# A dense block's norm steps put beside every second RWKV projection, and eight dense pieces moved into a gated product

## The reference

```python
# first block
o = diff_attention(...); y = gelu(s5_ssm(...))
y = y * sigmoid(y @ w_glu + b_glu)              # the gated product
y = rms_norm(y, ssm_out_g)
h_res = h_res + rms_norm(concat(o, y) @ w_out, post_mix_g)
h = rms_norm(h_res, pre_ffn_g)                  # "mix norm": both lines
f = (silu(h @ w_gate) * (h @ w_up)) @ w_down
x = h_res + rms_norm(f, post_ffn_g)
# second block
proj = rms_norm_2(x, norm_mix_w) @ w_in         # 14 tiles of RWKV columns, then retention
y = concat(retention(...), rwkv7_mix(...))
x = x + y @ w_o
x = x + (silu(rms_norm_2(x, norm_ffn_w) @ w_gate) * ...) @ w_down
```

## Time and profile before

| | us |
| --- | --- |
| median of 3 runs | 3587.25 (3585.57 to 3601.52) |
| the profiled execution | 3581.31 |
| its span, first to last instruction | 3579.3 |

### The profile page before, as it was taken

The page is one execution under the profiler, slowest core; times in us unless marked ns, Lnnn a source line. Parts: engine busy times, 40 slices in busy tenths (PEclk is TensorE's granted clock), DMA queues, the critical chain, the costliest instruction groups (busy, mean ns, idle before and its releaser), DMA issues.

```text
span 3579.3 us, 47875 instructions
## 1 busy us (share of the span) xinstructions
PE 3113.0 (87%) x19536; PEld 2394.1 (67%) x19536; DVE 1744.9 (49%) x2362; ACT 855.8 (24%) x1588; POOL 1969.1 (55%) x1076
## 2 busy tenths in 40 slices
PE   5977886699998768988999978988999989799997
PEld 4655564477776556766777766776777767688875
DVE  6733553443443552576666653286655564323233
ACT  3102112332222232122233223112222332200012
POOL 4801222255555464755676655665666674477873
PEclk9868997799999888999999999999999999899998
DMA  3334323122222233322222233432222221322331
GB/s 136 109 99 108 90 88 106 65 71 83 77 66 70 89 122 133 128 83 77 88 76 84 69 123 113 143 103 74 82 70 81 84 80 60 118 95 92 97 99 60
DMA packets 158027, 329.99 MB, mean 92 GB/s; under 512 B 34960, under 2 KB 74064, under 8 KB 157808
## 3 DMA queue, kind: packets, MB, share of 16 engines
q1 hardware_dynamic: 58752, 213.94, 18.6%
q10 hardware_dynamic: 99056, 112.99, 9.8%
HBM read 281.89 MB, written 44.97 MB: 91 GB/s over the span
## 4 chain that ended last, share of the span: by engine, by line
PE 71%; DVE 19%; ACT 3%; ACTq 2%; DMA 2%; issue 2%; DVEq 0%
PE ps L1778 30%; PE ps L1819 12%; PE ps L1807 12%; PE ps L1632 2%; DVE acc_dense L2219 2%; DVE ffh_lo L2903 1%; DVE act_lo L2219 1%; PE ps L1513 1%; DVE xn_dense L2226 1%; PE ps L2018 1%; ACTq L934 1%; PE ps L1553 1%; PE ps L1660 1%; DVE added L2219 1%; DVE turn L2219 1%
## 5 line engine op out<-in xcount | busy, mean ns | idle before, releaser
L537 POOL TENSOR_TENSOR w_hi<-w_raw,ones 128x1024 fp32r<-128x1024 f32 x408 | 795.0, 1949 | 1318.3 <-DMA w_raw<-weights 1304.3
L539 POOL TENSOR_TENSOR w_lo<-w_raw,w_hi 128x1024 fp32r<-128x1024 f32 x408 | 1006.6, 2467 | 32.0
L1778 PE MATMUL ps<-act_hi,w_hi 128*128 128x512 f32 x1696 | 702.6, 414 | 7.2 <-DVE act_lo L2219 6.6
L1778 PE MATMUL ps<-act_lo,w_hi 128*128 128x512 f32 x1696 | 676.7, 399 | 0.0
L1778 PE MATMUL ps<-act_hi,w_lo 128*128 128x512 f32 x1696 | 672.3, 396 | 0.0
L1778 PEld LDWEIGHTS ps<-act_hi,w_hi 128*128 128x128 f32 x1696 | 323.0, 190 | 99.1 <-issue 15.7
L1778 PEld LDWEIGHTS ps<-act_hi,w_lo 128*128 128x128 f32 x1696 | 322.8, 190 | 74.8
L1778 PEld LDWEIGHTS ps<-act_lo,w_hi 128*128 128x128 f32 x1696 | 322.8, 190 | 66.2 <-issue 1.7
L2219 DVE TENSOR_TENSOR acc_dense<-acc_dense,ps 128x512 f32<-128x512 f32 x352 | 242.0, 688 | 231.9 <-PE ps L1807 170.9
L1807 PE MATMUL ps<-w_hi,ffh_hi 128*128 128x512 f32 x704 | 293.7, 417 | 59.7 <-DVE acc_dense L2219 56.2
L1807 PE MATMUL ps<-w_hi,ffh_lo 128*128 128x512 f32 x704 | 279.7, 397 | 0.0
(11 more groups left out here) (374 smaller groups left out, 4482.9 us busy)
## 6 DMA issues: line engine op xcount, KB each, us to landing
w_raw<-weights SPq DMA_DIRECT2D x408, 512.0 KB, 3.5
rw<-rw_t ACTq DMA_DIRECT2D x24, 256.0 KB, 2.4
rw<-lora_t ACTq DMA_DIRECT2D x24, 256.0 KB, 2.0
row<-x ACTq DMA_DIRECT2D x8, 512.0 KB, 3.5
row_dense<-x ACTq DMA_DIRECT2D x8, 512.0 KB, 3.7
res<-row_dense ACTq DMA_DIRECT2D x8, 512.0 KB, 2.6
row_mix<-res ACTq DMA_DIRECT2D x8, 512.0 KB, 7.4
res<-row_mix ACTq DMA_DIRECT2D x8, 512.0 KB, 2.9
```

Source lines behind the costliest of these rows:

```text
L537: pool.tensor_tensor(w_hi[:, s], raw, ones[:, 0:1].to_broadcast([P, 1024]), MUL).then_inc(w_hi_made, 1)
L539: pool.tensor_tensor(w_lo[:, s], raw, w_hi[:, s].bitcast(F32), SUB).then_inc(w_ready, 1)
L1778: mm = pe.matmul(out, ws[w][:, s, P * k:P * k + P], acts[a][:, k, x], start=(k, w, a) == (0, 0, 0), stop=(k, w, a) == (KT - 1, 1, 0))
```

## The change

It does three things. The RWKV projection's six tiles move 16 KB further up in the mixing area, out of `acc_mix` and into the place of `row_mix` and `xn_mix`, which are done by then. In phase 1, attention's 68 steps carry 250 instead of 254 dense pieces, and the four steps of the gated product are followed by 12, 8, 4 and 20 pieces instead of 8, 4, 4 and 24. In phase 2, the six residual steps carry exactly the 32 pieces of `mix_product(1)`, and the six steps of `mix_norm(1)` come after RWKV projections 0, 2, 4, 6, 8 and 10, instead of all ahead of the first. In phase 3, the six steps of `dense_norm(3, 0)`, which came after projections 0 to 5, come after 0, 2, 4, 6, 8 and 10 as well. The order of the weight units doesn't change, nor does any instruction's size.

```diff
-    rw_t = place("rw_t", [P, 2, BANK], F32, AT_MIX)
-    lora_t = place("lora_t", [P, 2, BANK], F32, AT_MIX + 4096)
-    wa = place("wa", [P, BANK], F32, AT_MIX + 8192)
-    sgd = place("sgd", [P, BANK], F32, AT_MIX + 10240)
-    lora_w = place("lora_w", [P, 4 * P], F32, AT_MIX + 12288)
-    lora_g = place("lora_g", [P, 4 * P], F32, AT_MIX + 14336)
+    rw_t = place("rw_t", [P, 2, BANK], F32, AT_MIX + 16384)
+    lora_t = place("lora_t", [P, 2, BANK], F32, AT_MIX + 20480)
+    wa = place("wa", [P, BANK], F32, AT_MIX + 24576)
+    sgd = place("sgd", [P, BANK], F32, AT_MIX + 26624)
+    lora_w = place("lora_w", [P, 4 * P], F32, AT_MIX + 28672)
+    lora_g = place("lora_g", [P, 4 * P], F32, AT_MIX + 30720)
...
     def fills_heads(ahead, through, rest):
-        return [ahead] + spread(through - ahead, ATT_STEPS - 1) + [8, 4, 4, rest - through - 16]
-
-    FILLS = {1: fills_heads(8, 8 * HALF + NORM_STEPS + 224, len(first_starts)),
-             2: fills([10, 8, 6, 6, 4, 4], [0] * RW_TILES, len(first_starts)),
-             3: fills([5, 3, 3, 3, 8, 10], [1] * NORM_STEPS + [0] * (RW_TILES - NORM_STEPS), len(dense_starts))}
+        return [ahead] + spread(through - ahead, ATT_STEPS - 1) + [12, 8, 4, rest - through - 24]
+
+    FILLS = {1: fills_heads(8, 8 * HALF + NORM_STEPS + 220, len(first_starts)),
+             2: fills([8, 8, 6, 6, 4, 0], [1, 0] * NORM_STEPS + [0] * (RW_TILES - 2 * NORM_STEPS), len(first_starts)),
+             3: fills([5, 3, 3, 3, 8, 10], [1, 0] * NORM_STEPS + [0] * (RW_TILES - 2 * NORM_STEPS), len(dense_starts))}
```

## The result

| | before | after |
| --- | --- | --- |
| median, us | 3587.05 | 3626.83 (3619.27 to 3635.51, 4 runs) |
| the profiled execution | 3581.31 | 3619.27 |
| its span | 3579.3 | 3617.2 |

What follows compares the result with a forecast made beforehand. PE, busy 87% of the span, was taken as the bound, so only its idle time counted. 25.1 - 5.5 - 4 = +15.6 on 3581.31 gave 3596.9, as a median 3602.9; range for 8 in 10: 3576 to 3620.

Steps and rivals of the forecast that it cites:

- Part 1: Residual steps of phase 2: the first projection starts 33.8 us earlier; gain 34.8 us in all.
- The 1.0 us for a warm start: Phase 2's three first projections: starting warm, their 72 matmuls take 16.7 us instead of 17.76.
- Part 2: Mix norm among phase 2's projections: PE idles during the norm's ACT and DVE work; 59.9 us added, +25.1 net.
- step 0: First mix norm step among phase 2's projections: delays the second projection's sigmoid, 1 us.
- step 1: Mix norm step in phase 2 without a load of `x`: PE idles 10 us, 13 with the lower clock.
- Rival B: Phase 2's projections cover the norm, PE waits only 2.2 us in each of four steps: 3555; chance 0.12.
- Rival C: Phase 2's load of `x` is in time in steps 2 and 3, -4.7 each; Part 4 brings 11: 3587; chance 0.16.
- Part 3: Phase 3's dense norm: the first transposes' wait falls from 6.59 to 2.2 us and they run warm: -5.5 us.
- rival D: Phase 2's norm: DVE operations beside POOL's weight splits take 3.25 us instead of 1.28: +22, 3625; chance 0.20.
- Part 4: Phase 1's gated product: pieces taken from attention fill a PE wait, part given back: -4 us, bounds -11 to 0.
- the wait of 10.01: Gated product: PE waits for the down pieces behind ACT's 32 load issues; 5.6 us filled, down to about 4.4.

Runs made afterwards that it cites:

- phase 2 alone: Only the moved tiles and phase 2's new order, against the kernel before the change: ratio 1.0135 (1.0084 to 1.0186).
- PE's steps one later: Kernel with only phase 2 changed, but on PE each mix norm step stands one projection later than on ACT and DVE: 1.0008 against the kernel before.
- two later and with the loads early: Phases 2 and 3 changed, PE's mix norm steps two projections later, loads of `x` one step early: 0.9912 against the kernel before.
- the two edits done alone: Against the kernel before: gated product with 8, 8, 4, 20 pieces, 1.0023; attention with 250 pieces and gated product 12, 4, 4, 24, 1.0011.

## Why the prediction was wrong, point by point

- **Part 1** held: the first projection started 32.0 us earlier in phase 2 (predicted 33.8). Counted from the start of the phase, the second and fourth transposes came 1.5 and 1.2 us later than worked out; the wait ahead of the first projection was 3.38 (3.2). The 1.0 us for a warm start did not come: the first matmul ran at full speed, but the clock fell a microsecond later, and the 72nd matmul started 18.1 us behind the first, against 17.7 before.
- **Part 2** held: waits of 8.65, 14.66, 14.80 and 7.86 against 10, 14.7, 14.7 and 7 to 7.5, in sum +59.6 against +58.9. Part of that closeness is luck: step 0 cost 2.6 instead of 1, and step 1 less than forecast; with phase 2 alone the two are 0.8 and 9.87. The two orders (ACT behind PE's projection, PE behind ACT's norm) make most of the stall: PE's steps one later win 22.5 us of the 59.6, two later and with the loads early 48. Rival B, covered, fell. Rival C's load was 4.2 us a step, close to its 4.7, but not hidden in the change.
- **Part 3** had the right sign and the right wait; its size was 3.2, not 5.5. The first transposes waited 3.45 instead of 2.21 and were still at the lower clock (1.97). The 1.24 us between the two are DVE's shift standing beside POOL's split, rival D's mechanism at a place that the prediction didn't look at.
- **Part 4** is the step that failed: -4 forecast, +14.1 found. Its bounds, -11 to 0, excluded a loss, although the text named two mechanisms that could give one. "Delay DVE's squares by up to 3 us" was 5, the silu put the root 13.3 later, and with the longer last wait the gated product lost 6.0. And "if attention, where PE is bound, ends 5.6 earlier" did not hold: it ended 2.7 later, with the same matmuls at a lower clock. The 5.6 us to be filled at the wait of 10.01 were not won either: it fell to 8.86, and not to 4.4. Where the loss lies is shown by the two edits done alone; why the clock is lower under attention stays open.
- **Rival D** forecast 3625, and the median is 3626.8, but that is chance: in phase 2's steps 1 to 3 DVE's operations ran at 1.22 to 1.28, since POOL had no unit to split while PE stood still. Only step 4's `xn_dense` took longer, 2.35 beside a split.
- With the measured 14.1 instead of -4, the sum of the prediction is 25.1 - 5.5 + 14.1 = 33.7, against 37.9 in the spans. Parts 1 and 2 together were 2.5 short, part 3 2.3, and the untouched stretches gave 0.6 back. The upper end of the range, 3620, took 0 as the worst of part 4.

## What to carry to other kernels

Where several engines run hand-written lists, a step with a long chain over ACT and DVE is not "beside" the matmuls merely because it stands between them: put its PE part one or two matmul groups later than its ACT and DVE parts, and issue its loads a step ahead. When filler pieces are moved, look at which pieces become the last ahead of each waiting step and what they ask of the other engines, and give such an edit a bound on the losing side too. Compare stretches of the profile between fixed marks before believing a change of a few tenths of a per cent, and PE's idle time in them as well as their length: the clock alone moved an unchanged stretch of 112 us by 6.

## What the runs showed of the hardware

The granted clock is a cost of its own in a stage that PE nearly fills: 1935 matmuls took 440.5 us of busy time at 0.97 and 451.2 at 0.95, with no more idle time. The clock was not set by the waits alone: in phase 3's projections the same order with the same idle time of 15.7 to 16.0 us ran at 0.91 to 0.97, busy for 96.7 to 102.6. DVE operations with two SBUF inputs took up to 3.25 us beside a running POOL split and 1.23 to 1.28 without, and POOL's own operation grew from 2.4 to 3.2 in the same overlap. Size doesn't protect: an operation on one element per partition took 1.45 instead of 0.22, until POOL's had ended.
